# Two feed-forward ends of a two-block transformer kernel: who sums the squares, when the first half's root and tiles are made, and who writes the last output tiles

## The reference

```python
def rmsnorm(x, g):
    xf = x.astype(jnp.float32)
    r = lax.rsqrt(jnp.mean(xf * xf, axis=-1, keepdims=True) + EPS)
    return (xf * r * g.astype(jnp.float32)).astype(x.dtype)

# first block, end
h = h + (jax.nn.silu(m @ w_gate) * (m @ w_up)) @ w_down
# second block, start
a = rmsnorm(h, g_mix); proj = a @ w_in
# second block, end
h = h + (jax.nn.silu(gt) * up) @ w_down
return rmsnorm(h, g_final)
```

## Time and profile before

| what | us |
|---|---|
| median of 3 runs (2858.34 to 2860.44) | 2859.48 |
| the profiled execution, whole | 2857.05 |
| its span in the trace | 2854.9 |
| TensorE busy | 2759.4 (97%) |
| VectorE busy | 1580.7 (55%) |
| GpSimd busy | 1333.7 (47%) |
| ScalarE busy | 911.2 (32%) |

### The profile page before, as it was taken

One profiled execution on the slowest core, in us unless ns is written; L12 is line 12 of the kernel. 1 busy time (PEld: TensorE's weight loads), 2 busy tenths in 40 slices (PEclk: granted clock), 3 DMA queues, 4 the chain that ended last, 5 costly groups with the idle time before them and its releaser, 6 DMA issues. The chain is left out here.

```text
span 2854.9 us, 36940 instructions
## 1 busy us (share of the span) xinstructions
PE 2759.4 (97%) x13908; PEld 2231.2 (78%) x13908; DVE 1580.7 (55%) x2437; ACT 911.2 (32%) x1777; POOL 1333.7 (47%) x1012
## 2 busy tenths in 40 slices
PE   7999999999999999999999899999899999999997
PEld 6777788778888888787766688878787788888886
DVE  6776654865555555613367731243378655555556
ACT  5644431332222322324344410021243322223223
POOL 3322334466656666532222244546614665566653
PEclk9999999999999999999999999999999999999998
DMA  3010111112111111220111011132100111111111
GB/s 132 30 38 31 42 68 39 44 52 63 48 50 54 52 59 52 80 76 30 38 30 32 29 52 52 51 118 67 60 30 30 59 60 45 52 52 55 61 48 67
DMA packets 71376, 151.96 MB, mean 53 GB/s; under 512 B 6448, under 2 KB 29360, under 8 KB 70064
## 3 DMA queue, kind: packets, MB, share of 16 engines
q1 hardware_dynamic: 64256, 123.76, 13.6%
q10 hardware_dynamic: 6960, 26.01, 2.4%
HBM read 141.36 MB, written 8.39 MB: 52 GB/s over the span
## 5 line engine op out<-in xcount | busy, mean ns | idle before, releaser
L650 POOL TENSOR_TENSOR WH<-WRAW,CST 128x512 fp32r<-128x512 f32 x204 | 228.8, 1121 | 874.6 <-PE PS L775 750.1
L773 PE MATMUL PS<-XH,WH 128*128 128x512 f32 x1248 | 513.0, 411 | 2.8 <-DVE XL L2104 2.8
L775 PE MATMUL PS<-XH,WL 128*128 128x512 f32 x1248 | 489.7, 392 | 0.0
L774 PE MATMUL PS<-XL,WH 128*128 128x512 f32 x1248 | 489.0, 392 | 0.0
L684 POOL TENSOR_TENSOR WL<-WRAW,WH 128x512 fp32r<-128x512 f32 x216 | 309.9, 1435 | 272.7 <-ACT WH L1732 271.7
L2543 DVE TENSOR_TENSOR H<-H,PS 128x512 f32<-128x512 f32 x352 | 236.3, 685 | 161.7 <-PE PS L1097 159.3
L773 PEld LDWEIGHTS PS<-XH,WH 128*128 128x128 f32 x1248 | 235.3, 189 | 82.8 <-issue 36.3
L1095 PE MATMUL PS<-HH,WH 128*128 128x512 f32 x704 | 275.5, 391 | 5.3 <-DVE HL L2477 5.3
L1732 ACT ACTIVATE WH<-WRAW 128x512 fp32r<-128x512 f32 x204 | 129.4, 634 | 471.4 <-PE PS L1097 382.9
L652 POOL TENSOR_TENSOR WL<-WRAW,WH 128x512 fp32r<-128x512 f32 x204 | 271.6, 1331 | 16.0
L775 PEld LDWEIGHTS PS<-XH,WL 128*128 128x128 f32 x1248 | 235.4, 189 | 52.0
(11 more groups left out here) (334 smaller groups left out, 4989.4 us busy)
## 6 DMA issues: line engine op xcount, KB each, us to landing
WRAW<-ws SPq DMA_DIRECT2D x104, 512.0 KB, 3.5
WRAW<-ws SPq DMA_DIRECT2D x176, 256.0 KB, 2.6
RAWX<-ws SPq DMA_DIRECT2D x88, 256.0 KB, 2.7
H<-xT ACTq DMA_DIRECT2D x4, 1024.0 KB, 10.9
H<-xT ACTq DMA_DIRECT2D x2, 2048.0 KB, 11.0
h_spill<-H ACTq DMA_DIRECT2D x1, 4096.0 KB, 11.2
H<-h_spill ACTq DMA_DIRECT2D x4, 1024.0 KB, 8.0
outT<-H ACTq DMA_DIRECT2D x4, 1024.0 KB, 4.4
```

Source lines behind the costliest of these rows:

```text
L650: pool.tensor_tensor(WH[:, j, c], WRAW[:, j, c], ONES[:, 0:1].to_broadcast((P, 512)), ALU.mult).then_inc(hi_split, 1)
L773: pe.matmul(out, WH[:, j, w], rh(kt), start=(n == 0), stop=False)
L774: pe.matmul(out, WH[:, j, w], rl(kt), start=False, stop=False)
L775: last = pe.matmul(out, WL[:, j, w], rh(kt), start=False, stop=(n == len(kts) - 1))
```

## The change

It edits the last down step of both feed-forward parts and what follows.

1. GpSimd sums 14 squares instead of 8 (n = 0 to 13, into ACC[:, n // 8]); VectorE sums the last two.
2. TensorE does norm_sums of half 0 after o = 10 and norm_spread of half 0 after o = 12. Its norm_sums of half 1 comes right after o = 15 in the second part, and at kt == 3 of `first_units` in the first, with the spread of half 1 at kt == 6 instead of 3. The closing wait for h_added becomes two waits in `first_units`.
3. ScalarE loads the root's table at o == 0, takes the root of half 0 after o == 10, and makes the first three high parts after o = 13, 14, 15 (first part).
4. VectorE's reciprocal of half 0 comes after o == 11, and four scaled tiles (`early`) are made among o = 13, 14, 15 and the last two sums; in the second part these are four final tiles.
5. The last norm's tiles are shared: VectorE makes (0 to 4, half 1) and (0 to 3, half 0), GpSimd makes (4 to 7, half 0) and (5 to 7, half 1). For GpSimd, which reads SBUF, ScalarE first multiplies these tiles by the gain in place and copies the spread roots from PSUM to RFIN. The stores are three from ScalarE and three from SP.

```diff
@@ -336,7 +336,7 @@
         x_in2, bias_in0, bias_in1, sgu_in, mem_in = map(sem, ("x_in2", "bias_in0", "bias_in1", "sgu_in", "mem_in"))
-        h_out, y_out = map(sem, ("h_out", "y_out"))
+        h_out, y_out, y_out_pool = map(sem, ("h_out", "y_out", "y_out_pool"))
         x_part = [sem(f"x_part{q}") for q in range(4)]
@@ -375,7 +375,7 @@
             "mem_sq", "mem_sum", "mem_root", "mem_inv", "mem_spread", "mem_val", "mem_high", "mem_split"))
-        vm_turned, vm_copied, final = map(sem, ("vm_turned", "vm_copied", "final"))
+        vm_turned, vm_copied, final, final_pool, gained = map(sem, ("vm_turned", "vm_copied", "final", "final_pool", "gained"))
@@ -546,6 +546,10 @@
         U2V, VV, C21, C22 = (XX[:, HALF * n:HALF * (n + 1)] for n in range(4))
+        FINAL_POOL = [(kt, 0) for kt in range(4, 8)] + [(kt, 1) for kt in range(5, 8)]
+        RFIN = [XX[:, 0:HALF], XX[:, HALF:2 * HALF]]
@@ -637,6 +641,10 @@
             ffn(1, U_FFN2)
+            for kts, h, n in ((slice(4, 8), 0, 4), (slice(5, 7), 1, 6), (slice(7, 8), 1, 7)):
+                sp.wait_ge(final_pool, n)
+                sp.dma_start(outT[:, kts, half(h)], H[:, kts, half(h)]).then_inc(y_out_pool, 16)
+            sp.wait_ge(y_out_pool, 48)
@@ -735,10 +743,10 @@
                 base = 16 * (2 + 3 * f) - 12
-                for n in range(8):
+                for n in range(14):
                     pool.wait_ge(squared, base + n + 1)
                     pool.wait_ge(summed, base + n)
-                    pool.tensor_tensor(ACC[:, 0], ACC[:, 0], SQ[:, n % 2], ALU.add).then_inc(summed, 1)
+                    pool.tensor_tensor(ACC[:, n // 8], ACC[:, n // 8], SQ[:, n % 2], ALU.add).then_inc(summed, 1)
@@ -754,6 +762,11 @@
             ffn(1, U_FFN2)
+            for n, (kt, h) in enumerate(FINAL_POOL):
+                pool.wait_ge(rst_made, 3 + h)
+                pool.wait_ge(gained, n + 1)
+                x = H[:, kt, half(h)]
+                pool.tensor_tensor(x, x, RFIN[h], ALU.mult).then_inc(final_pool, 1)
@@ -793,11 +806,16 @@
                     lag = 3 if h or k == 3 or u0 == 0 else 0
+                    if k == 2:
+                        pe.wait_ge(h_added, 16 * DOWNS - 1 + h)
                     for m in range(KT + lag):
...
                                 continue
-                            if k is not None and h == 0 and u == u0 and kt == 3:
+                            if (k, h, u - u0, kt) == (2, 0, 0, 3):
+                                norm_sums(k, 1)
+                            if k is not None and h == 0 and u == u0 and kt == (6 if k == 2 else 3):
                                 norm_spread(k, 1)
@@ -1165,8 +1183,10 @@
                         last.then_inc(prod, 1)
-                        if ends and o == 11:
+                        if ends and o == 10:
                             norm_sums(k + 1, 0)
+                        if ends and o == 12:
+                            norm_spread(k + 1, 0)
@@ -1175,9 +1195,8 @@
                         down(b)
-                norm_spread(k + 1, 0)
-                norm_sums(k + 1, 1)
-                pe.wait_ge(h_added, 16 * DOWNS * (f + 1))
+                if f:
+                    norm_sums(k + 1, 1)
@@ -1466,7 +1485,7 @@
             def norm_root(k, h):
-                if h == 0:
+                if h == 0 and k not in (2, 5):
                     load_sqrt()
@@ -1479,7 +1498,7 @@
                 for n in range(first, last):
-                    if n == 2 and k != 3:
+                    if n == 6 and k != 3:
                         norm_root(k, 1)
@@ -1755,6 +1774,15 @@
+                def final_gain(n):
+                    kt, h = FINAL_POOL[n]
+                    x = H[:, kt, half(h)]
+                    act.activation(x, x, ACT.Copy, scale=v(V_GFIN + kt)).then_inc(gained, 1)
+                def final_roots(h):
+                    act.wait_ge(spread, 10 + h + 1)
+                    act.activation(RFIN[h], PS[:, OB + h], ACT.Copy).then_inc(rst_made, 1)
                 for n in range(16):
@@ -1806,13 +1834,23 @@
                         if b == DOWNS - 1:
+                            if o == 0:
+                                load_sqrt()
                             act.wait_ge(h_added, 16 * DOWNS * f + 16 * b + o + 1)
...
                             nsq.n += 1
-                            if o == 12:
+                            if o == 10:
                                 norm_root(k + 1, 0)
+                            if o >= 13 and not f:
+                                norm_high(2, o - 13, o - 12)
+                            if f and 8 <= o < 12:
+                                final_gain(o - 8)
+                            if f and o >= 13:
+                                final_gain(o - 9)
+                            if f and o == 12:
+                                final_roots(0)
                     if b < DOWNS - 1:
@@ -1822,7 +1860,6 @@
-            norm_high(2, 0, 3)
             act.dma_start(H_DRAM, H[:]).then_inc(h_out, 16)
@@ -2066,11 +2103,14 @@
             norm_root(5, 1)
-            for q in range(4):
-                h, kts = q // 2, slice(4 * (q % 2), 4 * (q % 2) + 4)
-                act.wait_ge(final, 4 * q + 4)
-                act.dma_start(outT[:, kts, half(h)], H[:, kts, half(h)]).then_inc(y_out, 16)
-            act.wait_ge(y_out, 64)
+            act.wait_ge(final, 4)
+            act.dma_start(outT[:, 0:4, half(0)], H[:, 0:4, half(0)]).then_inc(y_out, 16)
+            act.wait_ge(spread, 12)
+            act.activation(RFIN[1], PS[:, OB + 1], ACT.Copy).then_inc(rst_made, 1)
+            for kts, n in ((slice(0, 3), 7), (slice(3, 5), 9)):
+                act.wait_ge(final, n)
+                act.dma_start(outT[:, kts, half(1)], H[:, kts, half(1)]).then_inc(y_out, 16)
+            act.wait_ge(y_out, 48)
@@ -2111,12 +2151,12 @@
-            def norm_scale(k, gain):
-                for n in range(17):
+            def norm_scale(k, gain, first=0, last=17):
+                for n in range(first, last):
                     if n < 16:
                         kt, h = n % 8, n // 8
-                        if n == 2:
+                        if n == (6 if k == 2 else 2):
                             norm_inverse(k, 1)
@@ -2423,7 +2463,15 @@
-            def ffn(f, k, gain):
+            def final_norm(kt, h):
+                if kt == 0:
+                    dve.wait_ge(rst_made, 3 + h)
+                x = H[:, kt, half(h)]
+                dve.scalar_tensor_tensor(out=x, in0=x, scalar=v(V_GFIN + kt), in1=PS[:, OB + h], op0=ALU.mult,
+                                         op1=ALU.mult).then_inc(final, 1)
+            def ffn(f, k, gain, early):
                 hid, bases = 44 * f, N_DONE * f
@@ -2535,20 +2583,22 @@
                     base = 16 * (k + 1) + 4 - 16
-                    for o in range(17):
-                        if o < 16:
-                            t, h = down_tile(b, o)
-                            bank = o % 4 if ends else 4 + o % 4
-                            dve.wait_ge(prod, bases + DONE[kind, b, o])
-                            dve.tensor_tensor(H[:, t, half(h)], H[:, t, half(h)], PS[:, bank], ALU.add).then_inc(h_added, 1)
-                        if ends and o >= 9:
-                            if o == 9:
-                                dve.wait_ge(summed, base + 8)
-                            dve.wait_ge(squared, base + o)
-                            dve.wait_ge(summed, base + o - 1)
-                            dve.tensor_tensor(ACC[:, 1], ACC[:, 1], SQ[:, (o - 1) % 2], ALU.add).then_inc(summed, 1)
-                        if ends and o == 13:
+                    for o in range(16):
+                        t, h = down_tile(b, o)
+                        bank = o % 4 if ends else 4 + o % 4
+                        dve.wait_ge(prod, bases + DONE[kind, b, o])
+                        dve.tensor_tensor(H[:, t, half(h)], H[:, t, half(h)], PS[:, bank], ALU.add).then_inc(h_added, 1)
+                        if ends and o == 11:
                             norm_inverse(k + 1, 0)
+                        if ends and o in (13, 14, 15):
+                            early(o - 13)
+                    if ends:
+                        for n in (14, 15):
+                            dve.wait_ge(squared, base + n + 1)
+                            dve.wait_ge(summed, base + n)
+                            dve.tensor_tensor(ACC[:, 1], ACC[:, 1], SQ[:, n % 2], ALU.add).then_inc(summed, 1)
+                            if n == 14:
+                                early(3)
                     if not ends:
@@ -2557,10 +2607,8 @@
             residual(U_WO1, 1)
-            ffn(0, 1, V_F1)
-            norm_scale(2, V_GMIX)
+            ffn(0, 1, V_F1, lambda n: norm_scale(2, V_GMIX, n, n + 1))
+            norm_scale(2, V_GMIX, 4)
@@ -2774,17 +2822,10 @@
-            ffn(1, 4, V_GFFN)
-            for h in range(2):
-                dve.wait_ge(spread, 10 + h + 1)
-                for kt in range(KT):
```

(9 more changed lines are left out.)

## The result

The changed kernel takes 2866.61 us (median of 8 runs, 2865.14 to 2867.63), the kernel before 2858.46 in the same comparison (8 runs): **slower by 8.1 us, ratio 1.003, 95% interval 1.0019 to 1.0041**. The forecast was 2865.7, with a range of 2861.3 to 2868.3. The forecast change was +6.2, counted from an earlier median of the kernel before, 2859.48. The profiled execution took 2866.75 us with a span of 2864.7; before it was 2857.05 and 2854.9.

The account below looks back on a forecast made before the run. TensorE, busy for 97% of the span, was taken to bound the kernel, with the stores bounding its tail. First end +5.6 and second end +0.6 gave +6.2 us on the median 2859.48, so 2865.7, range 2861.3 to 2868.3.

Parts of the forecast that it names:

- The first end's chain: First end: 14 GpSimd sums delay the weight splits, TensorE waits, the stage ends at 1235.0 against 1229.4, +5.6 us.
- The third half: First end: third of four weight split halves on GpSimd, needed before the second matmul group; ready at 1208.5 instead of 1199.48.
- TensorE's slow stretch: First end: eight matmuls at 0.42 us after the idle time, seven at 0.23, 5.0 us in all, to 1213.5.
- The late spread: First end: spread of half 1 ends at 1219.45, holding VectorE's first tile of half 1; about 2 us of the +5.6.
- Rival 1: First end: GpSimd's splits take 2.36 us a half as when alone; +3.9, 2863.4, chance 0.22.
- Rival 2: First end: not slower, GpSimd through its sums by about 1194, late weights do not decide; 2857.2, chance 0.04.
- Rival 3: Second end: the two store queues overlap as at the kernel's start; -0.3 there, +5.3 in all, 2864.8, chance 0.10.
- Rival 4: Both ends: longer waits at GpSimd's halves (+1.2), more slow matmuls (+0.8), second end's upper bound (+0.6); +8.8, 2868.3, chance 0.14.
- its third term: Second end at its upper bound, +1.2: VectorE's sums slowed as at the first end, root 0.6 later; +0.6 on the forecast.
- The step that was mis-sized: Second end: last sum near 2841.2, root at 2842.4, ScalarE's first store at 2842.7, stores full behind it; end at 2855.5, +0.6 us.

Follow-up runs that it names:

- the first end alone: Kernel before with the change only at the end of the first feed-forward part; 2863.71 us, +4.8 on the kernel before.
- eight sums: Changed kernel, but in the first part GpSimd sums eight squares and VectorE the other eight; 2860.79 us, +1.9 on the kernel before.
- ScalarE's high parts: Changed kernel, but ScalarE instead of GpSimd makes the high parts of the four split halves; 2860.53 us, +2.3 on the kernel before.
- the lag: Changed kernel, but in half 0 of the first units too the second unit runs three kt behind the first; 2862.50 us, +3.6 on the kernel before.
- the two versions of the kernel before: Kernel before with the split halves' high parts on ScalarE, 2856.70 us (-1.7); the same with ten sums on GpSimd in the first part, 2858.59 us (+0.2).
- the kernel before with ScalarE's high parts: Kernel before with one edit, ScalarE makes the high parts of the four split halves; 2856.70 us, -1.7, ratio 0.9990.

## Why the prediction held, point by point

**The first end's chain** held link by link. The 14 sums of 1.42 were forecast to end at 1199.1: they ended at 1199.77, since the last waited 0.57 for its square. The third half was forecast at 1208.5, and 1208.80 was measured: the six split instructions took 9.1 us where 9.4 were counted, which gave back part of the late sums. TensorE's slow stretch, column sums, spread and VectorE's first tile of half 1 were forecast at 1219.45 (tile) and 1235.0 (end): 1220.10 and 1235.63. +5.6 was forecast, +6.0 measured in the profile, +4.8 in the medians of the first end alone. The kernels with eight sums, with ScalarE's high parts and with the lag each remove or shorten the wait by another means and give back 3.7 to 4.2 us of the 6.0, so that the late third half is the cause is shown. The late spread was forecast as about 2 us of it: 1.8 are left with the weights in time, and 1.63 of them are VectorE's wait for the spread.

**Rival 1** (splits at 2.36 a half) fell: 2.8 to 3.2 us a half. **Rival 2** (not slower) fell with the third half's time. **Rival 3** (the queues overlap) fell: 385 GB/s. The statement of the Trainium skill, page DMA: Bandwidth & Descriptors, section Issuing engines are not separate DMA queues, that copies from several engines interleave on the same 16 DMA engines, agrees with this. **Rival 4** (dearer) stood at +8.8, nearer to the measured +8.1 than the forecast was, but not by all its terms. No longer waits were seen at GpSimd's halves, and the 15 matmuls behind the third half took 5.1 us (1208.89 to 1213.99), where the forecast had 5.0. Only its third term came, the second end, and went past the +1.2 that was its upper bound.

**The step that was mis-sized** is the second end: "so its last sum ends near 2841.2", "**+0.6 us**", and "the stores stay full behind the first". The forecast stretched each of the two sums by up to 0.3 us beside GpSimd; they were stretched by 1.06 and 0.40, against 0.69 alone. (The terms written out for 2841.2 add up to 2840.7; five instructions and not four stand there, which gives about 2841.3.) And the root started 1.96 after the last sum (2846.16 against 2844.20), not the 1.23 taken over from before, since TensorE does the column sums at the low clock level by then. So the root came 27.0 us after the first sum of squares, where 25.1 was forecast, and with it the tiles of half 1 and the gap in the stores. The first store was not ScalarE's behind this root, as forecast, but SP's behind GpSimd's multiplies, which took 1.46 each, not 1.3 to 1.4. Together +2.5 instead of +0.6. By what the Trainium skill says on the page SBUF: State Buffer, section Summary: rules for kernel authors (a VectorE instruction with two SBUF inputs beside a GpSimd one that reads SBUF: the second to issue blocks until the first has finished), a sum of 0.69 could take up to 0.69 + 1.46 = 2.15, an estimate; the 1.75 lies under it. The prediction had used the milder rows of the first end.

**Luck.** The time came out 0.9 us above the forecast, the change 1.9 us (8.1 against 6.2). The forecast time was counted from a median of the kernel before that was 1.0 higher than the one of the comparison, and this hid about half of the miss.

## What to carry to other kernels

Before work is moved to an engine that looks idle, look at what is queued behind it there and when that is first needed: the third half was ready 5.5 us before TensorE began on the units, and six more sums took 9.0. VectorE's and GpSimd's times are not independent: beside GpSimd's reads of SBUF VectorE's sums took up to 1.75 us instead of 0.69, and GpSimd's splits 2.8 to 3.2 a half instead of 2.36, so work moved from VectorE to GpSimd comes back in part as stretch on both. Here the copy moved from GpSimd to ScalarE was the one edit that gained, and by little. A tail that the stores fill is shortened only if the last stores come sooner; an earlier first store left the queue empty later.

## What the runs showed that was not expected

The low clock at the start of the second part's last down step is not in every profile. TensorE waits 2.66 or 2.67 us there each time. In the profiles of before and of seven others it then runs at the low level for some matmuls; in those of the changed kernel, of the first end alone and of the two versions of the kernel before it does not. Two windows of the changed kernel, then one of the kernel before:

```profile
2817.00:2823.00 6.00, 4.73 (x21) 3.92 (x22) 5.00 (x7) 2.65 (x5) 0.67 (x1) 1.00 0.01 3
2838.00:2840.00 2.00, 2.00 (x6) 1.63 (x5) 0.57 (x2) 1.25 (x2) 1.86 (x2) 0.50 0.00 0
```

```profile
2811.00:2817.00 6.00, 4.92 (x15) 3.89 (x16) 4.89 (x7) 1.16 (x3) 0.48 (x1) 0.72 0.01 3
```

In the changed kernel's profile TensorE is then ahead of GpSimd's sums, waits 1.40 us for the eighth before its column sums, and the low level comes there instead (0.50 at 2838 to 2840). Its second end is 41.15, where the five kernels with the same second end and the low start have 39.8 to 40.1; that the clock makes this difference was argued from these rows and not tested. Against the three profiles of the old second end without the low start (36.70 and twice 36.96), 41.15 is 4.2 to 4.5 longer; against 37.55 with it, 40.06 is 2.5 longer.

The two profiles differ by 9.7 us in time and the medians by 8.1. This is the scatter of single executions: the profiled one of the kernel before is 1.4 below its median, that of the changed kernel 0.1 above. The stretch between the two ends, from the end of the first units to the second part's first sum, whose code is the same in all twelve kernels, takes 1587.9 us in both these profiles, so the 6.0 was passed on whole, but from 1586.2 to 1591.1 over the twelve. In the profile of the kernel before with ScalarE's high parts it is 1.6 longer, nearly what that edit gained at the first end. So a difference of a few us between the spans of two profiles says nothing by itself; the ends are compared from their own starts, and the whole by medians.
